# One attention routine for all four attentions: the order of VectorE and ScalarE, negated maxima, the scale in q, differential maps combined after the product with v

## What is computed

```python
sc = einsum('bhiqd,bhikd->bhiqk', qj, k) * scale      # i: two maps of a head
p = softmax(where(causal, sc, -inf), axis=-1)
w = p[:, :, 0] - lam * p[:, :, 1]
o = einsum('bhqk,bhkd->bhqd', w, v)
```

## Time and profile before

| | |
|---|---|
| three runs, median | 3347.1 us (3343.88 to 3348.02) |
| the profiled execution, span | 3352.8 us |
| diff, from its first scores to moba's | 65.0 us |
| moba | 30.5 us |
| nsa, layer 1 | 101.7 us |
| mla, layer 1 | 51.7 us |

### The profile page before, as it was taken

How to read it: one execution, slowest core, us unless ns; L and a number is a source line. 1 busy time by engine, 2 the same in 40 slices (tenths; PEclk the granted TensorE clock), 3 DMA queues, 4 the chain that set the end, 5 groups by cost and what they waited for, 6 DMA issues and landing times. The chain is left out here.

```text
span 3352.8 us, 65854 instructions
## 1 busy us (share of the span) xinstructions
PE 2825.7 (84%) x25476; PEld 2041.8 (61%) x25477; DVE 1291.4 (39%) x2922; ACT 898.9 (27%) x1856; POOL 280.1 (8%) x365
## 2 busy tenths in 40 slices
PE   6987675888888867989969597899999688899998
PEld 4965475444444423545538475778887566778886
DVE  1236554223222212333323474444443365643343
ACT  2233321112121101222213143343332133532232
POOL 1000000122221211222210100000000100000000
PEclk7996676899999967999989698999999788899999
DMA  6243006899999999799972300022221210022221
GB/s 181 77 154 117 1 13 252 318 385 344 382 386 387 344 391 388 241 353 386 361 260 84 96 1 26 26 76 101 101 101 60 69 51 1 26 73 85 95 101 50
DMA packets 299974, 581.92 MB, mean 174 GB/s; under 512 B 35780, under 2 KB 74372, under 8 KB 299764
## 3 DMA queue, kind: packets, MB, share of 16 engines
q1 hardware_dynamic: 279876, 557.27, 45.5%
q0 software_dynamic: 15792, 21.34, 2.9%
q10 hardware_dynamic: 4098, 0.49, 0.1%
HBM read 562.25 MB, written 16.78 MB: 173 GB/s over the span
## 5 line engine op out<-in xcount | busy, mean ns | idle before, releaser
L1909 PE MATMUL moe_up<-expert_w,mod 128*32 128x256 f32 x3856 | 243.1, 397 | 24.1 <-DMA expert_w<-in_exp_w_up 18.2
L1909 PE MATMUL moe_up<-ring,mod 128*32 128x256 f32 x3184 | 200.7, 402 | 30.9 <-issue 19.2
L1972 ACT ACTIVATE mod<-mod 128x128 f32<-128x128 f32 x158 | 48.9, 310 | 637.8 <-DVE mod L2004 637.8
L360 PE MATMUL mlp_bank<-hT_hi,mlp_w 128*128 128x512 f32 x512 | 199.4, 390 | 0.0
L362 PE MATMUL mlp_bank<-hT_hi,mlp_w 128*128 128x512 f32 x512 | 199.2, 389 | 0.0
L361 PE MATMUL mlp_bank<-hT_lo,mlp_w 128*128 128x512 f32 x512 | 199.2, 389 | 0.0
L360 PE MATMUL mlp_bank<-mlp_w,mlp_u_hi 128*128 128x512 f32 x512 | 199.2, 389 | 0.0
L361 PE MATMUL mlp_bank<-mlp_w,mlp_u_hi 128*128 128x512 f32 x512 | 199.2, 389 | 0.0
L362 PE MATMUL mlp_bank<-mlp_w,mlp_u_lo 128*128 128x512 f32 x512 | 199.2, 389 | 0.0
L1909 PEld LDWEIGHTS moe_up<-expert_w,mod 128*32 128x32 f32 x3856 | 122.7, 113 | 120.7 <-issue 27.1
L2002 DVE TENSOR_TENSOR mod<-moe_up,mod 128x256 f32<-128x256 f32 x158 | 67.1, 425 | 320.8 <-PE moe_up L1909 317.6
(11 more groups left out here) (522 smaller groups left out, 5765.1 us busy)
## 6 DMA issues: line engine op xcount, KB each, us to landing
expert_w<-in_exp_w_up SPq DMA_DIRECT2D x194, 512.0 KB
ring<-in_exp_w_up SPq DMA_DIRECT2D x150, 512.0 KB
ring<-in_w_ff SPq DMA_DIRECT2D x32, 2048.0 KB, 8.7
expert_w<-in_exp_w_down SPq DMA_DIRECT2D x47, 1024.0 KB, 11.1
ring<-in_exp_w_down SPq DMA_DIRECT2D x39, 1024.0 KB, 10.8
moe_w<-in_exp_w_up SPq DMA_DIRECT2D x74, 512.0 KB
ring<-in_ada_w SPq DMA_DIRECT2D x12, 2048.0 KB, 11.9
hT<-in_exp_w_up SPq DMA_DIRECT2D x48, 512.0 KB
```

The costliest lines, as they stand in the source:

```text
L360: nc.tensor.matmul(out, lhsT.hi, rhs.hi, start=(i == 0), stop=False)
L1909: mm = nc.tensor.matmul(up[half][quarter[q], 0:2 * UNITS], rowsT[:, f % 2, quarter[f // 2]], chunk[r][c][:, :, j, q * UNITS:(q + 1) * UNIT ...
L1972: nc.scalar.activation(sig[:, half], pre[:, half, 0:UNITS], ACT.Sigmoid, scale=ALPHA).then_inc(sig_ready, 1)
```

## The change

The routine loses its parameters `scale`, `pair`, `lam` and `gated`.

- The scale goes into q: the copies that turn q (`transpose_stage`) get a scale, 32 ** -0.5, 64 ** -0.5 or 96 ** -0.5. The exponential has none, and `compressed_attention_stage` adds its bias without it.
- The maximum is written negated by the reduction itself, and the product with -scale goes.
- DVE does maxima n+2, copy n+1, inverses n, output n. ACT does copy n+1, exponentials n+2.
- The differential maps are both turned and both multiplied with v. The inverse sums are multiplied by (1, -lam), a `gate`, and the output is p0 v * inv0 + p1 v * inv1, in two dependent instructions. `lam` becomes two columns, made in `lambda_stage`.
- moba and mla write both heads of a step with one instruction (`both_heads`).
- diff and moba become one stage, "mix", of 24 steps.

PE keeps its order. The core of the diff:

```diff
         @block.scalar
         def _(act):
             def exps(n):
...
                 if n >= 2:
-                    if pair:
-                        act.wait_ge(weights_ready, n - 1)
-                    else:
-                        act.wait_ge(turned, turns * (n - 1))
+                    act.wait_ge(turned, maps * (n - 1))
...
             def take(n):
+                b, nk = n % 2, keys(n)
+                if n >= 2:
+                    act.wait_ge(values_ready, n - 1)
+                act.wait_ge(turned, maps * n + 1)
+                nc.scalar.activation(pt[:, b, 0, 0:nk], tr[0][:, 0:nk], ACT.Copy).then_inc(taken_act, 1)
...
             exps(0)
+            take(0)
             exps(1)
-            take(0)
             for n in range(n_steps):
+                if n + 1 < n_steps:
+                    take(n + 1)
                 if n + 2 < n_steps:
                     exps(n + 2)
-                if n + 1 < n_steps:
-                    take(n + 1)
...
             def maxima(n):
...
                 dve.wait_ge(scores_ready, n + 1)
-                chain(nc.vector.tensor_reduce(top[:, b, :], sc[b][:, :, 0:nk], X, ALU.max))
                 if n >= 2:
                     dve.wait_ge(exp_ready, maps * (n - 1))
-                nc.vector.tensor_scalar(neg[:, b, :], top[:, b, :], -scale, None, ALU.mult).then_inc(bias_ready, 1)
+                nc.vector.tensor_reduce(neg[:, b, :], sc[b][:, :, 0:nk], X, ALU.max, negate=True).then_inc(bias_ready, 1)
...
-                if pair:
-                    chain(nc.vector.tensor_tensor(lam_inv[:, b, :], inv[:, c, 1:2], lam, ALU.mult))
-                    chain(nc.vector.tensor_scalar(p[:, b, 1, 0:nk], p[:, b, 1, 0:nk], lam_inv[:, b, :], None, ALU.mult))
...
-                    nc.vector.scalar_tensor_tensor(w[:, b, 0:nk], p[:, b, 0, 0:nk], inv[:, c, 0:1], p[:, b, 1, 0:nk],
-                                                   ALU.mult, ALU.subtract).then_inc(weights_ready, 1)
...
             maxima(0)
             maxima(1)
-            inverses(0)
             take(0)
             for n in range(n_steps):
-                if n + 1 < n_steps:
-                    inverses(n + 1)
                 if n + 2 < n_steps:
                     maxima(n + 2)
                 if n + 1 < n_steps:
                     take(n + 1)
+                inverses(n)
                 output(n)
...
+def both_heads(k, dst):
+    dst = dst.rearrange("p (m d) -> p m d", m=2)
+    def out(chain, psum, inv):
+        return k.nc.vector.tensor_tensor(dst, psum, inv.unsqueeze(2).to_broadcast(list(dst.shape)), ALU.mult)
...
-            chain(nc.vector.tensor_tensor(k.lam[:], e[:, 0:1], e[:, 1:2], ALU.subtract))
-            chain(nc.vector.tensor_scalar(k.lam[:], k.lam[:], LAM_INIT, None, ALU.add))
+            chain(nc.vector.memset(k.lam[:, 0:1], 1.0))
+            chain(nc.vector.tensor_tensor(k.lam[:, 1:2], e[:, 1:2], e[:, 0:1], ALU.subtract))
+            chain(nc.vector.tensor_scalar(k.lam[:, 1:2], k.lam[:, 1:2], -LAM_INIT, None, ALU.add))
...
-                def out(chain, psum, inv, m):
-                    return nc.vector.tensor_copy(tok[:, i, OUT_A + h * 64:OUT_A + (h + 1) * 64], psum)
+                def out(chain, psum, inv):
+                    chain(nc.vector.tensor_scalar(dst, psum[:, 0], inv[:, 0:1], None, ALU.mult))
+                    return nc.vector.scalar_tensor_tensor(dst, psum[:, 1], inv[:, 1:2], dst, ALU.mult, ALU.add)
...
-            attention_stage(k, "diff", [diff_step(h, i) for h in range(A_HEADS) for i in tiles(h)], A_DK ** -0.5, True, k.lam[:])
-            attention_stage(k, "moba", [moba_step(g, i) for g in range(2) for i in tiles(g)], B_DK ** -0.5, False)
+            attention_stage(k, "mix", [diff_step(h, i) for h in range(A_HEADS) for i in tiles(h)]
+                            + [moba_step(g, i) for g in range(2) for i in tiles(g)])
```

More of the change, by code:

```diff
@@ L744, in columns_of, with attention_stage @@
     return [src[:, t, c0:c0 + w] for t in range(NT)]
-def attention_stage(k, name, steps, scale, pair, lam=None, gated=False, last_key=None):
+def attention_stage(k, name, steps, last_key=None):
     nc = k.nc
     maps = 2
-    turns = 1 if pair else 2
     with ExitStack() as ctx:
@@ L769, in attention_stage @@
         p = sb("p", [P, 2, maps, S])
-        pt = sb("pt", [P, 2, turns, S])
-        w = sb("w", [P, 2, S]) if pair else None
-        top = sb("top", [P, 2, maps])
+        pt = sb("pt", [P, 2, maps, S])
         neg = sb("neg", [P, 2, maps])
@@ L781, in attention_stage, with keys @@
         n_steps = len(steps)
+        def keys(n):
+            return P * (steps[n].i + 1)
         @block.sync
@@ L823, in values @@
                     pe.wait_ge(out_taken, n - 1)
-                for m in range(turns):
-                    u = n * turns + m
-                    pe.wait_ge(taken_act if u % 2 == 0 else taken_dve, u // 2 + 1)
+                for m in range(maps):
+                    pe.wait_ge((taken_act, taken_dve)[m], n + 1)
                     for j in range(st.i + 1):
@@ L841, in _ @@
                 values(n)
[L843 to L849, removed]
-            if u % 2 == 0:
-                nc.scalar.activation(pt[:, b, m, 0:nk], tr[0][:, 0:nk], ACT.Copy).then_inc(taken_act, 1)
-            else:
-                nc.vector.tensor_copy(pt[:, b, m, 0:nk], tr[1][:, 0:nk]).then_inc(taken_dve, 1)
         @block.scalar
@@ L908, in inverses @@
                 dve.wait_ge(inverted, n + 1)
[L909 removed]
+                if st.gate is not None:
                     chain(nc.vector.tensor_tensor(inv[:, c, :], inv[:, c, :], st.gate, ALU.mult))
[L911 to L922 removed]
             def output(n):
[L925 removed]
                 dve.wait_ge(values_ready, n + 1)
[L927 to L929 removed]
+                steps[n].out(chain, ov[n % 2][:, 0:maps * 64].rearrange("p (m d) -> p m d", m=maps), inv[:, n % 4, :]).then_inc(out_taken, 1)
             maxima(0)
             maxima(1)
[L933 removed]
             take(0)
             for n in range(n_steps):
[L936 to L937 removed]
                 if n + 2 < n_steps:
@@ L2234, in compressed_attention_stage @@
     nc = k.nc
-    scale = DK2 ** -0.5
     with ExitStack() as ctx:
@@ L2349, in step, with out @@
             part = [slice(64 * g, 64 * g + 64) for g in range(G2)]
-            def out(chain, psum, inv, m):
-                h = m * R2 + r
-                dst = o[:, i, h * DK2:(h + 1) * DK2]
-                return nc.vector.scalar_tensor_tensor(dst, psum, inv, dst, ALU.mult, ALU.add)
+            def out(chain, psum, inv):
+                for m in range(2):
+                    dst = o[:, i, (m * R2 + r) * DK2:(m * R2 + r + 1) * DK2]
+                    last = nc.vector.scalar_tensor_tensor(dst, psum[:, m], inv[:, m:m + 1], dst, ALU.mult, ALU.add)
+                return last
             return Step(i=i, q=[qT[part[m], r, i * P:(i + 1) * P] for m in range(2)],
@@ L2358, in step @@
                         gate=gates[:, i, r:H2:R2, 1 + branch])
-        attention_stage(k, f"nsa{l}", [step(br, r, i) for br in range(2) for r in range(R2) for i in tiles(r)],
-                        DK2 ** -0.5, False, gated=True)
+        attention_stage(k, f"nsa{l}", [step(br, r, i) for br in range(2) for r in range(R2) for i in tiles(r)])
 def mla_stages(k, l, tok):
```

86 lines of the change are left out of this document (32 added, 54 removed).

## The result

The changed kernel takes 3294.8 us (median of 5 runs, 3277.7 to 3296.9) against 3347.1 us (5 runs, 3343.9 to 3348.6): a ratio of 0.9837, 95% interval 0.9817 to 0.9858. The forecast was 3294 us. The agreement is luck in part: it came out by two errors of opposite sign, and one of them is the more interesting half of this case.

What follows compares the result with a forecast made beforehand. PE was taken to bound nsa and mla, with diff at half clock. Savings of 26.8 (merged stage), 22.2 (nsa) and 4.6 (mla), less 0.5, made 53 us: 3294 us in the runs, range 3279 to 3325.

Steps and rivals of the forecast that it cites:

- The reordering: In nsa and mla, new DVE and ACT order cuts PE's idle: 22.2 us in two nsa, 4.6 in two mla.
- late turns on rising widths: In nsa, DVE is longer than PE on short steps, so turns of widths 2 to 4 come late: 0.4 us a period.
- the 3.7 us at half speed at the end: At nsa's end, 3.7 us return if shorter idle keeps the clock; half counted, 1.8 us per stage.
- mla, 2.3 each: In mla, 1.3 us from the last wait, 0.2 from the beginning, some 0.8 from the rest; 4.6 in two layers.
- The merged stage: Diff and moba as one stage at full clock, 68.7 us against 95.5: 26.8 us saved.
- Why full clock?: In the merged stage, the first wait shrinks from 3.6 to about 1.0 us, so PE's clock stays full.
- rival 2: Diff's steps in the merged stage stay at half speed, 34 us over forecast there: 3328 us; 16% with its half form.
- its weak form: Half of diff in the merged stage at half speed: 3311 us; within the 16% shared with the full form.
- Rival 1: Idle in nsa and mla only moves to another wait; only the merged stage's 26.8 us remain: 3320 us; 12%.
- Rival 3: Short steps of nsa and diff open gaps in which PE's clock falls every period, costing 172 us: 3466 us; 3%.
- rival 4: DVE's maximum still waits behind the previous output; nothing changes at w=4, at worst like rival 1; no separate chance.
- A rule and the rows: In diff, the rule that sustained activity releases the clock, against half speed for some 60 us with PE busy 81%.

Runs made afterwards that it cites:

- e7: The kernel before with only the new DVE and ACT order, in moba, nsa and mla; diff, negation, scales and outputs stay: 3309.1 us, ratio 0.9883.
- e8: The changed kernel with the products of the second scores of every attention stage done twice: 3280.5 us, ratio 0.9793.
- e2: The changed kernel with the old order put back on both DVE and ACT: 3315.0 us, ratio 0.9904.
- e10: The changed kernel once more, unchanged, run beside later variants and profiled: 3294.6 us, ratio 0.9851.
- e5: The changed kernel with diff and moba as two stages instead of one merged stage: 3300.2 us, ratio 0.9856.
- e6: The kernel before with PE's turn and product with v of every diff step done twice, DVE's combining kept: 3374.2 us, ratio 1.0081.
- e1: The changed kernel again, unchanged, for a second profile: 3286.4 us, ratio 0.9843.
- e3: The changed kernel with the old order put back on ACT alone, DVE's new: 3309.7 us, ratio 0.9911.
- e12: The changed kernel with moba's steps first in the merged stage and the old order on both DVE and ACT: 3309.7 us, ratio 0.9883.

## Why the prediction was right, and where it was not

**The reordering: right in mechanism, too small.** Forecast 11.1 us for each nsa, measured 13.9 and 12.3 (in the profile after). By its terms: the period was to be 21.0 to 21.1 and is 20.75. Of the late turns on rising widths that I walked out, 0.4 us a period, the first one is there, 0.15 us at width 2 where I had 0.16, inside the turn and not as a wait before it; those of widths 3 and 4 are not. In e7, with the negation still in DVE's way, they come to 0.23 more. From the last scores to the last turn I had 3.85 and it is 3.47. Of the 3.7 us at half speed at the end I counted half, and the whole of it came back, with 0.63 us of idle in place of 1.76, in nsa of both layers. mla, 2.3 each, gave 3.2 and 5.2; the second has a last product of 5.42 us before, which no row of mine had shown. Together nsa and mla gave 34.6 us where I had 26.8.

**The merged stage: forecast 68.7, found 65.8 in the profile after and 79.4 in a typical execution.** (The terms of the forecast add up to 68.8.) The step that failed is "Why full clock?". I took the fall in diff to come from the 3.6 us wait for the first combined weights, and held against it mla's gap of 0.9 us which left the clock at full. The wait did shrink to 1.07 us, and the clock falls there or close to it all the same, in seven of the eight traces that have diff in front; in e8 it falls without that wait, in e2 ahead of it. The term would have been right for the work: at full speed the stage takes 2.9 us less than I summed up. What it missed is 13.6 us lost in some 30 us of half speed, so it was a gain of 16.4 us in most executions and not of 26.8.

**So rival 2 was partly true.** I gave it 16% and called its weak form half of diff at half speed: 3311 us. In e10 about half of diff's 16 steps run at half speed, so this is what most executions do; my price for it was 17 us, the traces have 13.6. It did not end at 3311 because nsa and mla gave 35.8 us in e10 where I had 26.8, and because the work of the merged stage was 2.9 us less. The stages that I took as unchanged are 7.8 us shorter, which is of the size by which the profiled execution of before was a long one. Of these 5.2 lie between mla of layer 1 and nsa of layer 2, 584.2 us before and 579.0 in e10. The change need not be their cause: the same stretch took 584.0 us in e5, which has the change there, and 581.9 and 580.9 in e6 and e7, which have not.

**The other rivals.** Rival 1 (the idle moves to another wait) is out: no period of nsa has one, and nsa is 12 to 14 us shorter. Rival 3 (the clock falls in the gaps of the short steps) is out too, since there are none. What it feared may be what e6 shows, though: behind a wait of 0.83 us between steps PE is at half speed for the rest of the stage. That it doesn't do what it says (rival 4) is out by the earlier trace rows against the waits above.

**A rule and the rows.** One reading there was wrong: in diff before, PE's waits after the first one were 0.2 to 0.8 us, but the last turn's was 2.9 us. The rows of the changed kernel put the question without waits: the merged stage stood at 0.50 with PE busy 30.50 of 30.50 us in e10. The Trainium skill, TensorE: Matmul & The Clock Gate, section "The HAM clock gate", has it that the default is throttled and activity releases it. The trace agrees in so far as PE, busy all the time, did come back to full speed; but being busy does not settle when, as the same steps came back after 3.4 us in e1 and after 30.7 in e10.

**What stays open.** What makes the clock of the merged stage fall in one execution and not in the next, with the same waits in both, and why it is back after 3.4 us in e1, 6.8 in e8 and 31 to 34 in e10 and in e2 to e6. Whether what runs ahead of the stage has a part in it was not tried. Nor is there a cause for the single long runs, 3309.8 and 3312.7 us here and 3330.3 in e3. Shown is only that with moba's steps in front, or with doubled second scores, all 15 runs lie between 3276.6 and 3283.5 us.

## What to carry to other kernels

In a software pipeline on several queues, put first on each queue what the bounding engine waits for next, and last what only closes a step: here two queues with a few lines moved gave 40 us of 3347, and the merge and the new formula less. Count what a long wait at the end of a stage can cost twice, once as idle and once as the half-speed work behind it. And before a short profile is believed, take the spread of the runs and the clock of each: a profiled execution can be the best of two kinds.

## What the runs showed of the hardware

- PE can be busy without a pause and stay at half speed for 30 us (e10, 289.0 to 319.5), in steps with 32-row scores, and the same kernel was back after 3.4 us in another execution (e1). In the 64-row steps of the same routine it was back after 3.4 or 6.8 us in nsa, and 3.8 to 9.2 us after the first scores in a moba that began at half speed.
- The clock fell behind a wait of 0.83 us in e6, 3.4 us after it had come back, and inside unbroken work in e8, 1.7 us after the stage's first scores, while 11 waits of 0.38 us on average in nsa of e12, and waits of up to 0.67 us in nsa of the kernel before, left it at full.
- The product with v, 28 matmuls of 64 columns, costs 3.24 us at full and 6.07 at half speed, so a late turn at the end of a stage cost up to 3.7 us beside its wait (turn and product together, nsa before).
- Much of a program's spread can be the clock of one stage: the kernel before, at half speed in diff in its trace, spread over 10 us in 32 runs; the changed one over 35 us in 14, of which up to 14 are the merged stage's clock; with moba in front over 6 us in 10.
